# The first expert's weights chosen from half the tokens and loaded ahead of the routing plan, in a transformer layer with a mixture of experts

## The reference

```python
x = layer_norm(alpha * x + g1 * y, ln1_g[i], ln1_b[i])
x = layer_norm(alpha * x + g2 * hier_moe(modulate(x, sh2, sc2), *moe_w), ln2_g[i], ln2_b[i])

def hier_moe(h, w_rg, b_rg, w_re, b_re, w_gate, w_up, w_down):
    p_group = softmax(t @ w_rg + b_rg)                      # 4 groups
    p_g, grp = lax.top_k(p_group, 1)
    p_e, local = lax.top_k(softmax(logits_in), 2)           # 2 of the group's 8 experts
    gate = p_g * p_e / sum(p_e);  expert = grp * 8 + local
    # for each token, over its two experts: gate * (silu(x @ w_gate[e]) * (x @ w_up[e])) @ w_down[e]
```

## Time and profile before

| | |
|---|---|
| median of 3 runs | 1686.23 us (1686.06 to 1686.39) |
| the profiled execution | 1685.53 us |
| its span | 1683.70 us |
| TensorE busy | 1518.9 us, 90% |
| VectorE busy | 928.1 us, 55% |
| ScalarE busy | 693.9 us, 41% |
| GpSimd busy | 210.7 us, 13% |
| read from and written to HBM | 256.41 MB, 45.67 MB |

### The profile page before, as it was taken

How to read it: one execution, slowest core, us unless ns; L and a number is a source line. 1 busy time by engine, 2 the same in 40 slices (tenths; PEclk the granted TensorE clock), 3 DMA queues, 4 the chain that set the end, 5 groups by cost and what they waited for, 6 DMA issues and landing times. The chain is left out here.

```text
span 1683.7 us, 47319 instructions
## 1 busy us (share of the span) xinstructions
PE 1518.9 (90%) x19673; PEld 1126.3 (67%) x19673; DVE 928.1 (55%) x1855; ACT 693.9 (41%) x1585; POOL 210.7 (13%) x274
## 2 busy tenths in 40 slices
PE   5799998999977899986999989998999999998868
PEld 2578886779967888874666668887656565665433
DVE  6798762342115556648989957865151553444416
ACT  5444431012234454534767745532242433533311
POOL 0000000000034445314000000000000000000015
PEclk9799999999988999997999989999999999999989
DMA  9312224542133334213011024417858789999976
GB/s 369 113 63 94 93 86 159 202 157 76 50 106 118 110 117 138 88 53 122 20 44 51 7 92 176 163 66 306 347 190 340 279 330 418 413 419 419 364 246 250
DMA packets 115267, 305.34 MB, mean 181 GB/s; under 512 B 11010, under 2 KB 57682, under 8 KB 106074
## 3 DMA queue, kind: packets, MB, share of 16 engines
q1 hardware_dynamic: 93178, 244.95, 38.6%
q0 software_dynamic: 10336, 46.67, 7.8%
q10 hardware_dynamic: 11520, 10.49, 2.0%
HBM read 256.41 MB, written 45.67 MB: 179 GB/s over the span
## 5 line engine op out<-in xcount | busy, mean ns | idle before, releaser
L2767 PE MATMUL psum<-now_hidden,i_xm 128*32 128x256 f32 x4992 | 289.7, 384 | 13.4 <-DVE now_hidden L2877 12.4
L2767 PEld LDWEIGHTS psum<-now_hidden,i_xm 128*32 128x32 f32 x4992 | 161.0, 111 | 124.6 <-DVE now_hidden L2877 17.4
L2779 PE MATMUL psum<-now_down,i_hT 128*32 128x256 f32 x2464 | 148.8, 382 | 5.6 <-ACT now_down L2834 5.3
L2893 DVE TENSOR_TENSOR i_h<-i_silu,psum 128x128 f32<-128x128 f32 x78 | 22.4, 287 | 203.2 <-ACT i_silu L2827 201.5
L2779 PEld LDWEIGHTS psum<-now_down,i_hT 128*32 128x32 f32 x2464 | 80.2, 111 | 60.8 <-ACT now_down L2834 7.2
L2877 DVE COPY now_hidden<-raw_hidden 128x1024 f32 x168 | 104.6, 695 | 27.3 <-DMA raw_hidden<-in_w_up 19.1
L2817 ACT ACTIVATE i_xm<-psum,run_mod 128x128 f32<-128x128 f32 x163 | 63.0, 453 | 122.2 <-issue 83.2
L124 PE MATMUL psum<-hT_head,wm_head 128*128 128x512 f32 (+1 forms) x256 | 96.9, 379 | 11.2 <-DVE hT_rest L415 6.9
L1924 PE MATMUL psum<-dkT,f_qT 64*128 64x512 f32 (+1 forms) x384 | 89.7, 575 | 17.2 <-ACT f_E L1974 14.8
L1974 ACT ACTIVATE f_E<-psum,f_mx 128x1280 f32<-128x1280 f32 (+2 forms) x96 | 92.8, 971 | 18.8 <-DVE f_mx L2035 17.9
L124 PE MATMUL psum<-hT_head,wm_rest 128*128 128x512 f32 (+1 forms) x256 | 95.2, 372 | 0.0
(11 more groups left out here) (380 smaller groups left out, 3079.1 us busy)
## 6 DMA issues: line engine op xcount, KB each, us to landing
raw_hidden<-in_w_gate SPq DMA_DIRECT2D x22, 2048.0 KB, 24.0
raw_hidden<-in_w_up SPq DMA_DIRECT2D x22, 2048.0 KB, 30.9
raw_down<-in_w_down SPq DMA_DIRECT2D x22, 2048.0 KB, 21.2
wa_late<-in_w_ada POOLq DMA_DIRECT2D x16, 1024.0 KB, 5.7
yb<-i_y ACTq DMA_DIRECT2D x80, 128.0 KB, 10.4
wa<-in_w_ada SPq DMA_DIRECT2D x8, 1024.0 KB, 13.6
wt<-in_w_in SPq DMA_DIRECT2D x4, 2048.0 KB, 9.2
wm<-in_w_in SPq DMA_DIRECT2D x12, 512.0 KB, 4.3
```

Source lines behind the costliest of these rows:

```text
L2767: last = nc.tensor.matmul(by_blocks(hidden_bank(s)[j * SUB:(j + 1) * SUB, :]), xm[u][:, k, s * SUB:(s + 1) * SUB], columns_of(now["hidden" ...
L2779: last = nc.tensor.matmul(down_bank(s)[j * SUB:(j + 1) * SUB, :], hT[s % 2][:, k * SUB:(k + 1) * SUB], now["down"][:, k, j * WIDE:(j + 1) ...
```

## The change

The first expert is picked from the picks of tiles 0 to 3. In `mixed_output` TensorE counts these with one product, in front of the second half of tile 7; VectorE (`pick_first`) takes the expert with most of them, writes its number and its one-hot; SP loads its gate and up weights before it stores tile 7 (`load_first`), into slot 2, which `w_route` leaves for an address lower down. At the start of `routing` SP loads its down weights, in front of six small transfers. ScalarE copies both into `now` during the routing; the copies at L2916 and L2859 go. The expert's key gets 100000 more, so that it stands at place 0. When the plan is written, SP issues the loads of place 1 alone.

The row numbers of the picks are now summed in TensorE's memory: seven products with ones for the tiles before, and one with the starts of the experts, in place of `upto_tile`, `rank` and `base`. `placed` is one instruction in place of two, `part_hot` one in place of two, `row_hot` three (4, 6 and 6 picks) in place of two. The counts of spare transposes are others.

The diff, cut to its core (left out: declarations, line breaks, and the same renaming of slots in `hidden_slot`):

```diff
+        self.first_hot, self.first = m.sb("r_first_hot", [P, NE]), m.sb("r_first", [P, 1], I32)
@@ -2094,7 +2095,10 @@
...
-    w_route = m.sb("w_route", [P, KD, NG + NE])
+    w_route = nc.alloc_sbuf_tensor_at("w_route", [P, KD, NG + NE], F32, offset=m.high - 4 * KD * P)
+    m.keep["raw_loaded"] = {n: [m.sem(f"w_{n}_loaded{u}", lasting=True) for u in range(k)] for n, k in (("hidden", SLOTS), ("down", 2))}
+    choice = m.keep["choice"]
+    early_chosen, early_counted, first_known = (m.sem("g_" + n) for n in ("early_chosen", "early_counted", "first_known"))
@@ -2151,6 +2157,8 @@
                 if t:
                     store_x1(t - 1)
                     store_xn(t - 1)
+            sp.wait_ge(first_known, 1)
+            load_first(m, sp, "hidden")
             store_x1(TL - 1)
             store_xn(TL - 1)
@@ -2257,6 +2265,18 @@
                 dve.wait_ge(x_normed, TL - 1)
...
+            def pick_first():
+
+                number = m.keep["small"][:, COUNT:COUNT + NE]
+                dve.wait_ge(early_counted, 1)
+                link(nc.vector.tensor_reduce(early_total[:, :], m.bank(7, TL // 2 * NE, 2 * P).rearrange("p (t e) -> p e t", e=NE), AX, ALU.add))
+                link(stt(early_key[:, :], early_total[:, :], float(NE), number, ALU.mult, ALU.subtract))
+                link(nc.vector.tensor_reduce(early_top[:, :], early_key[:, :], AX, ALU.max))
+                link(nc.vector.tensor_scalar(choice.first_hot[:, :], early_key[:, :], early_top[:, :], None, ALU.is_equal))
+                link(tt(early_own[:, :], choice.first_hot[:, :], number, ALU.mult))
+                link(nc.vector.tensor_reduce(early_at[:, :], early_own[:, :], AX, ALU.add))
+                nc.vector.tensor_copy(choice.first[:, :], early_at[:, :]).then_inc(first_known, 1)
@@ -2269,7 +2289,10 @@
...
-                    m.keep["choice"].choose(dve, 0, TL // 2)
+                    choice.choose(dve, 0, TL // 2)
+                    dve.sem_inc(early_chosen, 1)
+                if t == TL - 1:
+                    pick_first()
                 add(t, 1)
@@ -2307,7 +2330,7 @@
...
-            def route(t):
+            def route(t, turns_between=0):
@@ -2317,6 +2340,8 @@
                     pe.wait_ge(route_loaded, 16)
                 for k in range(KD):
                     last = nc.tensor.matmul(m.bank(6, NG + NE), h2T[t % 2][:, k, :], w_route[:, k, :], start=(k == 0), stop=(k == KD - 1))
+                    if k < KD - 1:
+                        spare_turns(m, turns_between)
                 last.then_inc(routed, 1)

@@ -2325,12 +2350,17 @@
...
                 if t >= 2:
                     route(t - 2)
+                if t == TL - 1:
+                    pe.wait_ge(early_chosen, 1)
+                    nc.tensor.matmul(m.bank(7, TL // 2 * NE, 2 * P), m.keep["ones"], choice.M[:, 0:TL // 2, :].rearrange("p t e -> p (t e)").bitcast(F32),
+                                     start=True, stop=True).then_inc(early_counted, 1)
                 project(t, 1)
                 if t:
                     turn_x(t - 1)
-            spare_turns(m, 25)
-            route(TL - 2)
-            spare_turns(m, 14)
+            pe.wait_ge(first_known, 1)
+            spare_turns(m, 29)
+            route(TL - 2, 1)
+            spare_turns(m, 6)
             turn_x(TL - 1)
             spare_turns(m, 11)
             route(TL - 1)
@@ -2339,7 +2369,21 @@
...
-    return (place + 1) % SLOTS
+    return SLOTS - 1 - place % SLOTS
+
+
+def load_first(m, sp, part):
+
+    raw, loaded = m.keep["raw"], m.keep["raw_loaded"]
+    e = sp.value_load(m.keep["choice"].first[0:1, 0:1], min_val=0, max_val=NE - 1)
+    if part == "hidden":
+        for w, n in enumerate(("gate", "up")):
+            src = m.dram[f"w_{n}"].rearrange("e (a p r) n -> e p a (r n)", p=P, r=RUN)
+            dst = raw["hidden"][:, slot_of(0), w, :, :].rearrange("p (a r) n -> p a (r n)", r=RUN)
+            sp.dma_start(dst, one(src, e).rearrange("e p a n -> (e p) a n")).then_inc(loaded["hidden"][slot_of(0)], 16)
+    else:
+        src = m.dram["w_down"].rearrange("e (k p) n -> e p k n", p=P)
+        sp.dma_start(raw["down"][:, 0, :, :], one(src, e).rearrange("e p k n -> (e p) k n")).then_inc(loaded["down"][0], 16)
@@ -2422,11 +2466,13 @@
...
+    lowered, numbered, split = m.sem("r_lowered"), m.sem("r_numbered"), m.sem("r_split")
+    PARTS = ((0, 4), (4, 10), (10, PICKS))
...
     @block.sync
     def _(sp):
+        load_first(m, sp, "down")
         for j in range(SUBS):
             here = d["mod_rows"][5:6, j * (D // SUBS):(j + 1) * (D // SUBS)]
             sp.dma_start(rep_g[j * SUB:(j + 1) * SUB, :], here.to_broadcast([SUB, D // SUBS])).then_inc(gate_loaded, 16)
@@ -2434,9 +2480,8 @@
...
         sp.wait_ge(planned, 1)
-        for place in range(2):
-            for part in expert_loader(m, sp, place, place):
-                part()
+        for part in expert_loader(m, sp, 1, 1):
+            part()
@@ -2474,6 +2519,7 @@
...
         link(stt(key[:, :], nblk[:, :], 2.0 * NE, number, ALU.mult, ALU.subtract))
+        link(stt(key[:, :], choice.first_hot[:, :], 1.0e5, key[:, :], ALU.mult, ALU.add))
@@ -2486,6 +2532,7 @@
...
         column(nblk_col[:, :], nblk[:, :])
+        link(ts(nblk_col[:, :], nblk_col[:, :], float(SUB), None, ALU.mult))
@@ -2503,19 +2550,11 @@
...
         link(stt(closed[:, :], pos[:, :], ids[:, 0:1], number, ALU.is_equal, ALU.mult))
         red(lists[:, 0:1], closed[:, :], AX, ALU.add).then_inc(ordered, 1)
-        link(nc.vector.memset(upto_tile[:, 0, :], 0.0))
-        for t in range(TL - 1):
-            link(tt(upto_tile[:, t + 1, :], upto_tile[:, t, :], m.bank(1, NE, t * NE), ALU.add))
         dve.wait_ge(order_turned, 1)
         cp(plan[0:1, PLAN_EXPERT:PLAN_EXPERT + NE], m.psum[0:1, 6 * NC:6 * NC + NE]).then_inc(planned, 1)
-        link(tt(rank[:, :, :], m.bank(0, TL * NE).rearrange("p (t e) -> p t e", e=NE), upto_tile[:, :, :], ALU.add))
-
-        dve.wait_ge(based, 1)
-        link(ts(base[:, :], m.bank(4, NE), float(SUB), None, ALU.mult))
-        link(tt(rank[:, :, :], rank[:, :, :], base[:, :].unsqueeze(1).to_broadcast([P, TL, NE]), ALU.add))
-        for j in range(2):
-            last = tt(placed[:, j, :, :], choice.E[:, j, :, :], rank[:, :, :], ALU.mult)
-        link(last)
+        dve.wait_ge(numbered, 1)
+        numbers = m.bank(0, TL * NE).rearrange("p (t e) -> p t e", e=NE)
+        link(tt(placed[:, :, :, :], choice.E[:, :, :, :], numbers.unsqueeze(1).to_broadcast([P, 2, TL, NE]), ALU.mult))
         link(red(rowf[:, :, :], placed[:, :, :, :], AX, ALU.add))
@@ -2523,18 +2562,20 @@
...
-        link(stt(in_part[:, :], part_of[:, :], -float(P), flat_row, ALU.mult, ALU.add))
+        stt(in_part[:, :], part_of[:, :], -float(P), flat_row, ALU.mult, ALU.add).then_inc(split, 1)
         link(tt(is_part[:, :, :], each_pick(part_of[:, :], QUADS),
                 small[:, COUNT:COUNT + QUADS].unsqueeze(1).to_broadcast([P, PICKS, QUADS]), ALU.is_equal))
-        for j in range(2):
-            here = slice(j * TL, (j + 1) * TL)
-            tt(part_hot[:, here, :], is_part[:, here, :], ids[:, :].unsqueeze(2).to_broadcast([P, TL, QUADS]), ALU.mult)
-            tt(row_hot[:, here, :], in_part[:, here].unsqueeze(2).to_broadcast([P, TL, P]),
-               small[:, COUNT:COUNT + P].unsqueeze(1).to_broadcast([P, TL, P]), ALU.is_equal).then_inc(picked, 1)
+        every_id = ids[:, :].unsqueeze(1).unsqueeze(3).to_broadcast([P, 2, TL, QUADS])
+        tt(part_hot[:, :, :].rearrange("p (j t) q -> p j t q", j=2), is_part[:, :, :].rearrange("p (j t) q -> p j t q", j=2), every_id, ALU.mult)
+        dve.wait_ge(split, 1)
+        for a, z in PARTS:
+            tt(row_hot[:, a:z, :], in_part[:, a:z].unsqueeze(2).to_broadcast([P, z - a, P]),
+               small[:, COUNT:COUNT + P].unsqueeze(1).to_broadcast([P, z - a, P]), ALU.is_equal).then_inc(picked, 1)

...
-        link(tt(ends[:, :], m.bank(4, NE), nblk[:, :], ALU.add))
+        dve.wait_ge(based, 1)
+        link(stt(ends[:, :], m.bank(4, NE), 1.0 / SUB, nblk[:, :], ALU.mult, ALU.add))
@@ -2565,10 +2606,16 @@
...
         last.then_inc(rounded, 1)
+        act.wait_ge(loads["hidden"][slot_of(0)], 32)
+        for k in range(KD):
+            nc.scalar.activation(now["hidden"][:, :, k, :], raw["hidden"][:, slot_of(0), :, k, :], ACT.Copy).then_inc(copied["hidden"], 1)
         act.wait_ge(chosen, 1)
         nc.scalar.activation(eg[:, :, :], eg[:, :, :], ACT.Exp).then_inc(act_did, 1)
         act.wait_ge(lowered, 1)
         nc.scalar.activation(v["e2"][:, :], v["e2"][:, :], ACT.Exp).then_inc(act_did, 1)
+        act.wait_ge(loads["down"][0], 16)
+        for k in range(KE):
+            nc.scalar.activation(now["down"][:, k, :], raw["down"][:, 0, k, :], ACT.Copy).then_inc(copied["down"], 1)
@@ -2578,24 +2625,29 @@
...
         nc.tensor.matmul(m.bank(1, TL * NE), ones, every, start=True, stop=True).then_inc(counted, 1)
```

(21 more changed lines are left out.)

13 lines of the change are left out of this document (7 added, 6 removed).

## The result

| | before | changed |
|---|---|---|
| median of six executions | 1685.47 us | 1695.74 us |
| ratio, 95% interval | | 1.0044 [1.0027, 1.0062] |
| the profiled execution: time, span | 1685.53, 1683.70 us | 1689.26, 1687.1 us |
| granted clock, mean of the span | 0.963 | 0.958 |

The changed kernel is slower by 0.44%, some 7 us, and outside the range. The ratio, like all ratios here, leaves out disturbed executions, here one of the changed kernel with 2509.7 us; without it the median would be 1695.60, so the ratio is not the quotient of the medians, which would be 1.006. Its profiled execution is the shortest of its six, so the trace shows less of the loss than the timing does; that is taken up at the end.

What follows compares the result with a forecast made beforehand. TensorE and DMA were taken to alternate as limits in the experts stage, which shifts as one piece. The terms 0.2 - 0.3 - 1.3 + 0 + 1.7 = +0.3 us on 1686.23 gave 1686.5 us, range 1681.9 to 1689.4.

Steps and rivals of the forecast that it cites:

- What bounds the kernel: Experts stage: TensorE and DMA alternate, the stage shifts as one piece; block 0 waits for gathered tokens, not weights.
- Part 1: End of the mixed output: stores behind the early load set the barrier, +0.2 us, bounds -0.6 and +1.6.
- Part 2: Weights of place 0: copies moved to ScalarE are hidden, the wait at the first down product goes, -0.3 us.
- Part 3: The plan's chain on VectorE gets shorter, -1.3 us, bounds -0.9 and -1.7.
- Part 4: The gather before block 0 again takes 8.3 us to land, 0 change, bounds -2.0 and +4.6.
- Rival (c): Gather before block 0 gets slower behind expert weights, 12.9 us, sum +4.9, 1691.1 us; chance 12%.
- Rival (b): Gather lands in 6.3 us, clock at block 0 holds, stores delay nothing: -4.2, 1682.0 us; chance 24%.
- Part 5: Block 0: TensorE idles 4 to 7 us after 22 spare transposes and loses clock, +1.7 us, bounds 0 and +1.7.
- The chances: Whole kernel: faster by over 0.2% 0.25, slower 0.13, within 0.62.

Runs made afterwards that it cites:

- b_same: The kernel before, unchanged, timed and profiled again: 1685.99 us, ratio 0.9992.
- a_stores_first: Changed kernel with SP storing x1 and xn of tile 7 before it issues the early load: 1687.67 us, ratio 1.0017.
- a_again: The changed kernel, unchanged, timed a second time: 1690.65 us, ratio 1.0041.
- a_turns60: Changed kernel with 60 spare transposes in front of block 0 in place of 22: 1687.40 us, ratio 1.0008.
- a_turns84: Changed kernel with 84 spare transposes in front of block 0 in place of 22: 1685.63 us, ratio 0.9998.
- a_gather_first: Changed kernel with SP waiting for the first two gathers before it loads the weights of place 1: 1682.74 us, ratio 0.9986.
- b_turns22_again: Kernel before with 22 spare transposes in front of block 0 in place of 56, second timing: 1691.34 us, ratio 1.0034.
- b_plan: Kernel before with the new plan chain alone, no early pick or load, 56 spare transposes in front of block 0: 1686.72 us, ratio 1.0007.
- a_both: Changed kernel with tile 7's stores ahead of the early load and 84 spare transposes in front of block 0: 1685.65 us, ratio 0.9993.
- a_third: The changed kernel, unchanged, timed a third time: 1689.36 us, ratio 1.0026.
- a_gather_best: Changed kernel, gather before place 1's loads, tile 7's stores before the early load, 24 spare transposes before the count, 36 before block 0: 1682.04 us, 0.998.

## Why the prediction was wrong, by its own steps

**What bounds the kernel: right.** The experts stage was only shifted, block 0 waited for tokens and not for weights, and the expert was the same one.

**Part 1: the term that failed.** I put the early load and the stores at +0.2 us with +1.6 as the bound. The mean of the changed executions is +2.2 over those of before, and +2.7 over `b_same` alone; `a_stores_first`, which differs only in SP's order, takes 3.1 off. The bytes were right. The DMA view from 1115 to 1133 us:

```profile
DMA packets 584, 5.26 MB, mean 292 GB/s; under 512 B 70, under 2 KB 70, under 8 KB 327
```

5.26 MB, where I had 5.24. What was wrong is the rate and the base. The stores were done some 1.0 us before 1133.12, at 1132.1, that is 16.4 us after the load's issue at 1115.68 and not 14.3: 320 GB/s, while I had taken the 363 of a stretch with loads alone. In two stretches of 2 us, the second after both stores had been issued, the engines were no less busy and moved less:

```profile
1121.12:1123.12 2.00, 2.00 (x21) 2.00 (x22) 1.90 (x4) 0.00 (x0) 0.00 (x0) 1.00 1.05 451
...
1125.12:1127.12 2.00, 1.83 (x17) 1.59 (x15) 1.33 (x4) 1.33 (x4) 0.00 (x0) 1.00 1.10 295
```

That stores cause this is argued, not shown; in `a_again` the slow stretch (223 GB/s) had a DMA share of 0.77, so there the engines weren't all busy. The load's issue was as I had said: 1.2 us later in this trace (1114.5), but so was tile 6's store ahead of it (1112.85 against 1111.68), and in `a_again` it went out at 1114.51. The sum that I had kept as the upper bound was the right one. It took one landing of the second load, 13.2 us, and 2.5 us for the stores behind it, which puts the barrier at 1131.65 and A at 20.0 us; A was 19.9 to 20.3 in the changed kernel. `a_again` has both rows, the load issued at 1114.97 and the store at 1122.83, so they landed at 1128.1 and 1130.5, 2.5 us apart:

```profile
raw_hidden<-in_w_up SPq DMA_DIRECT2D x1, 2048.0 KB, 13.1
...
xn<-g_xn SPq DMA_DIRECT2D x1, 512.0 KB, 7.7
```

So I had the landing in a row and took the mean rate of a stretch over it. That the measured +2.2 lies above the +1.6 comes from the base: 18.42 us was slow by 1.1 against `b_same`, and the +2.2 is counted from the mean of both. The Trainium skill says (DMA: Bandwidth & Descriptors, "Queues, rings and completion order") that each pair of queue row and DMA engine is a ring of its own, and that the engine takes turns between the rows it has work for. The trace agrees that stores on SP's queue do not pass its loads: the wait was 7.0 us behind them and 0.3 in front of them.

**A wait that I had not priced.** I let the barrier shift everything after it. In five of the changed kernel's relatives (`a_again`, `a_turns60`, `a_turns84`, `a_stores_first`, `a_gather_first`) the 42 spare transposes ahead of the count ran at the lower clock, took over 7 us in place of 4.78, and the count began 1.3 to 1.6 us late. They were counted as free, which these 42 are at the full clock (1.00, 2.4 GHz) only. A term of 0 to +1.6 was missing. Whether all of it belongs to the change is open, since `b_turns22_again`, the kernel before up to that place, had 6.44 us and a count that was 0.4 us late.

**Part 2: right in kind, too small.** The wait at the first down product and the late SiLU are gone: where the clock was full D is 15.64 to 15.74 against 16.29, so -0.6 us, where I had -0.3.

**Part 3: right in sign, outside its bounds.** Where the count was on time within 0.2 us, B was 1.8 to 2.3 us shorter (22.25, 22.33, 22.13, 21.90), against -1.3 and a bound of -1.7. The step that was off is the plan's copy: it came 14.24 us after the barrier (13.88 in `b_plan`) against 14.80, so -0.6 to -0.9 where I had -0.2. The two added operations cost 0.2 us each, as charged: the reduction to `r_lists` started 12.99 us after the barrier before, and 13.41 in `a_both`, whose count was on time. What I had too small is the removal of the additions behind it: from that reduction to the plan's copy it was 1.8 us before and 0.7 after, so -1.1 where I had -0.6. The reduction of `placed` follows the copy after 0.80 us, about the 0.9 I had; so it came 1.8 us sooner (15.04 against 16.82), and the rest of B took 7.21 us against 7.34.

**Part 4: right.** 8.7, 8.2 and 8.1 us against 8.3. Rival (c) fell: no gather came near 11.4. Rival (b) fell as well, since no gather met only the tail of the weights. I gave its -2.0 as the bound for a gather with no load in flight. The row that I took, 6.3 us at 1236.35, had no weights beside it but four stores of 128 KB, and the DMA share was 0.63; with nothing in flight it is nearly -4, as `a_gather_first` shows with 4.5 us.

**Part 5: right in kind, too small in the trace and far too small in the timed runs.** TensorE idled 4.58 us; the hidden products took 5.10 (predicted 5.3). But I had counted only the hidden products of block 0. The eight transposes ahead of them, on the path too, took 1.95 in place of 1.13, +0.8; D rose by 2.1, or by 2.7 with the -0.6 of Part 2 taken out, against 1.7. The timed cost of 22 in place of 56 is some 5 us by two timings of the kernel before; with 84 in their place the changed kernel's ratio goes down to 0.9998 from 1.0026, 1.0041 and 1.0044.

**What stays open.** The stretches explain +2.7 us of profiled time; the ratios say +4.4 to +7.4. The same gap stands in both runs of the kernel before with 22, where the weights are loaded as before, so at least there it comes with the missing spare transposes and not with the weights. The granted clock of each timed execution bears on it. Its mean over the span (the profiled executions of the tried kernels left out) was lower by 0.0019 and 0.0046 in the kernel before with 22 than in the kernel before beside it, by 0.0034 and 0.0037 in `a_again` and `a_third`, and higher by 0.0013 in the changed kernel with 84. Among the executions of the kernel before itself, 23 to 35 in a session, the time rises by 1.0 to 1.1 us for each 0.001 that the mean clock is lower. By that, as an estimate, 22 in the kernel before cost 2 and 5 us, where the timed loss is 5 and 5.7. So the clock accounts for much of the gap and not surely for all. The mean is no measure of time by itself, since it counts idle stretches too: `a_gather_best` had 0.9608 where the kernel before beside it had 0.9627, and was the faster. Nor do the stretches cover what lies upstream: tile 6's store went out at 1113.2 us on average in the four profiles of the kernel before and of its version with 22, and at 1115.2 in the eleven of the changed kernel and its versions, with a scatter of several us in each, so a cost there is neither shown nor ruled out. The timed executions are not profiled, so where in them the clock is low isn't known.

**The chances.** I gave 0.13 to slower, 0.12 of it to a slow gather. The mechanisms that decided, a late barrier and a lost clock, were both in my sum, each with a bound that was a single row. What was missing is a rival for the two beyond their bounds: the change leaves TensorE idle for 3.8 us and more twice, each time the work after it began at half rate, and the timed cost of the 22 alone is some 5 us where the bound on the clock was 1.7.

## What to carry over

Before a large load is put on a queue, look at what small transfer stands behind it and what barrier waits for that; its place in the order cost 3 us of the trace here and nothing else changed with it. Spare TensorE work ahead of a wait must be sized anew whenever the wait's start or end moves: too few cost more (22 for 56: 0.3%) than too many (84: 1.4 us of overrun, and still 0.4% better than 22). And when a load becomes early, ask which later load has lost its urgency: holding back place 1's weights until the gather had landed halved the gather, kept the clock at block 0, and took the changed kernel from 1689.36 to 1682.74 us, a gain of 0.4% like that of the 84.

## What was not expected of the hardware

- A gather of the same rows took 4.5 and 4.6 us with no other transfer in flight, and 8.1 to 8.7 us beside 2 MB weight loads. The Trainium skill (DMA: Bandwidth & Descriptors, "Queues, rings and completion order") says that DMA engines take turns between queue rows by the packet; that the gather, on GpSimd's queue, is slowed and not stopped agrees with it.
- After 3.8 to 6.6 us of idle TensorE began at a granted clock of 0.50, and stayed there for some us while it worked. The changed kernel, in stretches of 2 us from the barrier on:

```profile
1133.12:1135.12 2.00, 2.00 (x10) 2.00 (x11) 1.73 (x9) 2.00 (x4) 0.00 (x0) 0.50 0.27 33
1135.12:1137.12 2.00, 2.00 (x16) 2.00 (x15) 1.73 (x9) 2.00 (x3) 0.00 (x0) 0.77 0.74 256
1137.12:1139.12 2.00, 2.00 (x22) 2.00 (x19) 1.43 (x7) 2.00 (x3) 0.00 (x0) 1.00 1.02 416
```

- The same instructions after the same idle time ran at 0.50 in one execution and at 1.00 in another. In `a_stores_first` and `a_both`, which differ only behind them, the 42 took 7.64 and 4.78 us after 1.12 us of idle. Two executions of one program, the kernel before with 22 at block 0, have them at

```profile
1133.14 4.77 PE L1731 MATMUL psum<-mask 128*128 128x128 f32 x42 [1.25 <-PEq L3054]
...
1127.75 6.44 PE L1731 MATMUL psum<-mask 128*128 128x128 f32 x42 [1.25 <-PEq L3054]
```

The clock at a given instruction is not a property of the program alone, and a stretch that has it once in one trace may not have it in the next: the 14 transposes of the earlier trace rows, 3.23 us there and 1.73 in `b_same`, misled the prediction in just this way.
